# Splitting an attention pair's softmax into three places of the issue order, with two norms applied in other ways

## The reference

```
h  = rms(x) * ln1_g * (1 + sc1) + sh1;   u = h @ w_in
fox: 8 heads of 64:  logit = q.k/8 + cum[t] - cum[s], causal; softmax; @ v      (cum: running sum of log sigmoid)
diff: 4 heads:       (softmax(q1 k1 + alibi) - lam * softmax(q2 k2 + alibi)) @ v, then rms over 128
x  = x + g1 * (concat(fox, diff) @ w_out)
h2 = rms(x) * ln2_g * (1 + sc2) + sh2;   x = x + g2 * ((silu(h2 @ w_gate) * (h2 @ w_up)) @ w_down)
```

## Time and profile before

| | us |
|---|---|
| median of 3 runs | 817.25 |
| the profiled execution, whole | 818.92 |
| its span, first to last instruction | 817.2 |
| PE busy, matmuls | 775.0 (95%) |
| DVE busy | 466.4 (57%) |
| ACT busy | 390.6 (48%) |
| POOL busy | 59.4 (7%) |

### The profile page before, as it was taken

How to read it: one execution, slowest core, us unless ns; L and a number is a source line. 1 busy time by engine, 2 the same in 40 slices (tenths; PEclk the granted TensorE clock), 3 DMA queues, 4 the chain that set the end, 5 groups by cost and what they waited for, 6 DMA issues and landing times.

```text
span 817.2 us, 10224 instructions
## 1 busy us (share of the span) xinstructions
PE 775.0 (95%) x3955; PEld 616.8 (75%) x3955; DVE 466.4 (57%) x607; ACT 390.6 (48%) x544; POOL 59.4 (7%) x70
## 2 busy tenths in 40 slices
PE   3988899988999999999999999999999999999995
PEld 2667675656888889888878887777888888888884
DVE  3466676747565556464595436555565656545364
ACT  3255666644344334353634356665455545335252
POOL 2004030010000000000280000000010000000001
PEclk9999999999999999999999999999999999999998
DMA  9998336895655347656749464333565645564601
GB/s 275 289 361 274 112 105 254 312 397 195 219 194 184 125 155 232 232 180 203 255 162 331 155 205 154 105 104 111 170 194 162 200 156 201 164 201 154 206 26 51
DMA packets 86785, 158.73 MB, mean 194 GB/s; under 512 B 5226, under 2 KB 23875, under 8 KB 84690
## 3 DMA queue, kind: packets, MB, share of 16 engines
q1 hardware_dynamic: 84562, 151.16, 55.7%
q0 software_dynamic: 2128, 6.90, 2.7%
q10 hardware_dynamic: 48, 0.01, 0.0%
HBM read 156.99 MB, written 1.08 MB: 193 GB/s over the span
## 4 chain that ended last, share of the span: by engine, by line
PE 82%; DVE 5%; issue 3%; SPq 3%; ACT 3%; DMA 2%; POOL 1%; DVEq 0%; POOLq 0%; ACTq 0%
PE PS L872 25%; PE PS L874 24%; PE PS L873 24%; PE PS L986 3%; DMA raw<-in_w_ada 2%; PE PS L1066 1%; ACT whi L1165 1%; PE PS L960 1%; DVE wlo L1377 1%; PE PS L1037 1%; SPq L802 1%; PE PS L1092 1%; PE PS L1021 1%; SPq L790 1%; POOL hrs L1780 1%
## 5 line engine op out<-in xcount | busy, mean ns | idle before, releaser
L1377 DVE TENSOR_TENSOR wlo<-raw,whi 128x2048 fp32r<-128x2048 f32 (+1 forms) x126 | 280.2, 2226 | 190.4 <-ACT whi L1165 162.4
L1165 ACT ACTIVATE whi<-raw 128x2048 fp32r<-128x2048 f32 (+1 forms) x126 | 227.1, 1804 | 156.2 <-PE PS L874 156.2
L872 PE MATMUL PS<-whi,hT 128*128 128x512 f32 (+1 forms) x704 | 280.6, 399 | 2.2 <-issue 1.9
L874 PE MATMUL PS<-whi,hT 128*128 128x512 f32 (+1 forms) x704 | 272.8, 388 | 0.0
L873 PE MATMUL PS<-wlo,hT 128*128 128x512 f32 (+1 forms) x704 | 272.7, 387 | 0.0
L872 PEld LDWEIGHTS PS<-whi,hT 128*128 128x128 f32 x704 | 133.5, 190 | 33.1 <-issue 8.4
L874 PEld LDWEIGHTS PS<-whi,hT 128*128 128x128 f32 x704 | 133.3, 189 | 27.5
L873 PEld LDWEIGHTS PS<-wlo,hT 128*128 128x128 f32 x704 | 133.7, 190 | 23.9
L872 PE MATMUL PS<-whi,hidT 128*128 128x512 f32 x216 | 84.5, 391 | 0.0
L874 PE MATMUL PS<-whi,hidT 128*128 128x512 f32 x216 | 84.1, 389 | 0.0
L873 PE MATMUL PS<-wlo,hidT 128*128 128x512 f32 x216 | 84.1, 389 | 0.0
(11 more groups left out here) (227 smaller groups left out, 643.7 us busy)
## 6 DMA issues: line engine op xcount, KB each, us to landing
raw<-in_w_in SPq DMA_DIRECT2D x36, 1024.0 KB, 5.1
raw<-in_w_ff SPq DMA_DIRECT2D x32, 1024.0 KB, 5.2
raw<-in_w_ada SPq DMA_DIRECT2D x16, 1024.0 KB, 6.9
raw<-in_w_gate SPq DMA_DIRECT2D x10, 1024.0 KB, 5.4
raw<-in_w_up SPq DMA_DIRECT2D x10, 1024.0 KB, 5.1
raw<-in_w_down SPq DMA_DIRECT2D x10, 1024.0 KB, 5.2
raw<-in_w_ada SPq DMA_DIRECT2D x16, 512.0 KB, 7.2
raw<-in_w_out SPq DMA_DIRECT2D x8, 1024.0 KB, 5.1
```

Source lines behind the costliest of these rows:

```text
L872: pe.matmul(o, ah, wh, start=(k == 0), stop=False)
L874: return pe.matmul(o, al, wh, start=False, stop=end)
L1165: act.activation(split_view(whi, i), slab_view(raw, slot, i), ACT.Copy).then_inc(hi_made, 1)
L1377: dve.tensor_tensor(split_view(wlo, i), slab_view(raw, slot, i), whole(split_view(whi, i)), ALU.subtract).then_inc(lo_made, 1)
```

## The change

1. A pair's `scores` step is cut in three. The maxima stay in `scores`; the exponentials on ACT become `exp u+1`, which is put behind `probsT u` (in fox behind its first head) and ahead of `heads u+2`; the reciprocals and the scaling on DVE become `probs u`, which is put at the front of pair u, ahead of `scores u+1`. For pair 0, `exp` stands behind `heads 1`.
2. The row constant `cumq` is gone: the `cum` step with its transposes and copy, and L1588 and L1589.
3. `lam` moves from behind `heads 1` to ahead of the forget gate.
4. The diff norm is done for heads 0 and 1 at the end of pair 6, and for heads 2 and 3 at the end of pair 7. The first `turn` stands directly behind pair 7.
5. Norm 1: POOL makes the root per half of the tokens, DVE scales the identity by it (`diag`), and PE multiplies x by `diag`, which transposes and scales in one; `xnb` is no longer made. `mod` is done in two parts, the first inside the output projection.
6. One slab's split is moved from the output projection to behind the last `turn` of norm 1.

The diff at its core (the rest declares and removes names, and counts `norm_rs` one lower):

```diff
@@ -140,17 +140,25 @@
         for u in us:
             moba, c = kind_of(u) == "moba", BETWEEN.get(u, BETWEEN[kind_of(u)])
 
+            out += [("probs", u)]
             if u != us[-1]:
                 out += [("scores", u + 1)]
             if moba and u != us[0]:
                 out += [("back", u - 1)]
-            out += fill(c[0]) + [("probsT", (u, 0))] + ([("probsT", (u, 1))] if moba else []) + fill(c[1])
+            out += fill(c[0]) + [("probsT", (u, 0))] + ([("probsT", (u, 1))] if moba else [])
+            if u != us[-1]:
+                out += [("exp", u + 1)]
+            out += fill(c[1])
             if u + 2 <= us[-1]:
                 out += [("heads", u + 2)]
             out += fill(c[2])
             if kind_of(u) == "fox":
                 out += [("probsT", (u, 1))] + fill(c[3])
             out += [("values", u)] + fill(c[4])
+            if u == FOX_P + 2:
+                out += [("diffnorm", 0)]
+            if u == FOX_P + 3:
+                out += [("diffnorm", 1)] + turns("diff", 0, (0,))
...
-    order += early + [("fgate", 0), ("unit", 0), ("logf", 0), ("unit", 1)]
+    order += early + [("lam", 0), ("fgate", 0), ("unit", 0), ("logf", 0), ("unit", 1)]
     now = whole("fox", 2, "w_in", 2 * W, "h")
-    order += insert(now, (4, early), (5, [("cum", 0)]), (6, [("heads", 0)]))
+    order += insert(now, (4, early), (6, [("heads", 0)]))
...
-    order += [("scores", 0), ("heads", 1), ("lam", 0)] + tail[:3]
+    order += [("scores", 0), ("heads", 1), ("exp", 0)] + tail[:3]
     tail = tail[3:]
     order += attention(list(range(FOX_P + DIFF_P)), tail, ada[18:20])
-    order += [("diffnorm", 0)] + ada[20:21] + turns("diff", 0, (0, 1)) + ada[21:22]
-    order += slab(wo[0], "w_out", 0, 4) + [("evac", wo[0])]
+    order += ada[20:22] + turns("diff", 0, (1,)) + insert(slab(wo[0], "w_out", 0, 4), (2, [("mod", 1)])) + [("evac", wo[0])]
     order += insert(slab(wo[1], "w_out", W, 4), (1, [("sums", (1, 0))])) + [("evac", wo[1]), ("sums", (1, 1))] + ada[22:24]
-    order += [("mod", 2), ("norm", 1)]
-    order += turns("norm", 1, (0, 1)) + parts("norm", 1, (0, 1)) + turns("norm", 1, (2, 3)) + parts("norm", 1, (2, 3))
+    order += [("norm", 1), ("first", 0), ("mod", 2), ("first", 1)]
+    order += turns("norm", 1, (0, 1)) + parts("norm", 1, (0, 1)) + [("first", 2), ("first", 3)]
+    order += turns("norm", 1, (2, 3)) + [("split", None)] + parts("norm", 1, (2, 3))
...
@@ -265,7 +273,8 @@
             split += 1
             continue
         if it[0] == "piece" and it[1]["first"] and it[1]["slab"] >= KC + 2:
-            while split <= min(it[1]["slab"] + min(2, it[1]["slab"] + 1), len(slabs) - 1):
+            held = tiles[it[1]["T"]]["name"] == "w_out" and it[1]["k"] == 4 and tiles[it[1]["T"]]["n"] == 1
+            while split <= min(it[1]["slab"] + (1 if held else 2), len(slabs) - 1):
                 out.append(("split", split))
...
@@ -965,13 +973,22 @@
 
                 elif kind == "mod":
 
-                    for n, pk in enumerate((1, 2)):
-                        pe.wait_ge(mod_in, pk)
-                        take(4 + n)
-                        for c in range(4):
-                            last = pe.transpose(PS[:, 4 + n, c * P:(c + 1) * P], mod[:, pk, c * P:(c + 1) * P], ident)
+                    pe.wait_ge(mod_in, i)
+                    take(3 + i)
+                    for c in range(4):
+                        last = pe.transpose(PS[:, 3 + i, c * P:(c + 1) * P], mod[:, i, c * P:(c + 1) * P], ident)
                     last.then_inc(mod_T, 1)
-                    reader[4] = reader[5] = [(ab_made, 1)]
+                    reader[3 + i] = [((b2_made, ab_made)[i - 1], 1)]
+
+                elif kind == "first":
+
+                    key = ("norm", 1, i)
+                    b = turn_bank(TURNS[key])
+                    take(b)
+                    pe.wait_ge(diag_made, 1)
+                    for c in range(2):
+                        k = 2 * i + c
+                        pe.matmul(PS[:, b, c * S:c * S + P], x[:, 0, k * P:(k + 1) * P], diag[:, 0, :], start=True, stop=True)
 
...
-                    for c in range(2):
-                        for t in range(TB):
-                            o = c * S + t * P
-                            last = pe.transpose(PS[:, b, o:o + P], src[:, t, c * P:(c + 1) * P], ident)
+                    if is_affine(i):
+                        for c in range(2):
+                            last = pe.matmul(PS[:, b, c * S + P:(c + 1) * S], src[:, 1, c * P:(c + 1) * P], diag[:, 1, :],
+                                             start=True, stop=True)
...
+                    dve.wait_ge(norm_rs, 1)
+                    dve.tensor_scalar(xn1[:, 1, :], x[:, 1, :], nrs[:, 0, 1:2], None, ALU.mult).then_inc(xn_dve, 1)
+
+                elif kind == "norm" and i == 1:
+                    for t in range(TB):
+                        dve.wait_ge(rs1_made, t + 1)
+                        dve.tensor_scalar(diag[:, t, :], ident, nrs[:, 1, t:t + 1], None, ALU.mult).then_inc(diag_made, 1)
...
                                 dve.wait_ge(setup_in, 16 * NSETUP)
-                                dve.wait_ge(cumq_in, 1)
-                            if a >= 2:
-                                dve.wait_ge(smax, 2 * (a - 2) + 2)
-                            dve.tensor_scalar(mcum[:, a % 2, 0:P], mask[:, P:2 * P], cumq[:, 0, a:a + 1], None, ALU.add)
-                            dve.tensor_scalar(mcum[:, a % 2, P:3 * P], mask, cumq[:, 1, a:a + 1], None, ALU.add
-                                              ).then_inc(mcum_in, 1)
-                            dve.wait_ge(mcum_in, a + 1)
-                            bias = [mcum[:, a % 2, c0:c1] for c0, c1 in QB]
+                            bias = [mask[:, P:2 * P], mask]
...
                             dve.tensor_tensor_reduce(made, score, bias[t], -1.0, 3e38,
                                                      ALU.add, ALU.min, nmax[:, a, t:t + 1]).then_inc(smax, 1)
+
+                elif kind == "probs":
+                    u, kd, sc = i, kind_of(i), scores_sb(i)
                     for n in range(2):
...
 
                 elif kind == "diffnorm":
-                    dve.wait_ge(drs_made, 1)
-                    dve.wait_ge(od_in, DIFF)
-                    o = od.rearrange("p t (h d) -> p (t h) d", h=DIFF)
-                    dve.tensor_tensor(o, o, spread(drs[:, :], P), ALU.mult).then_inc(od_made, 1)
+                    dve.wait_ge(drs_made, i + 1)
+                    dve.wait_ge(od_in, 2 * i + 2)
+                    o = od[:, :, i * 2 * P:(i + 1) * 2 * P].rearrange("p t (h d) -> p t h d", h=2)
+                    rs = drs[:, 2 * TB * i:2 * TB * (i + 1)].rearrange("p (h t) -> p t h", h=2)
...
@@ -1809,6 +1820,13 @@
 
                 elif kind == "norm":
                     n = i
+                    if n == 1:
+                        for t in range(TB):
+                            pool.wait_ge(sums_made, 3 + t)
+                            then(pool.tensor_tensor(nss[:, 1, t:t + 1, 0], nss[:, 1, t:t + 1, 0], nss[:, 1, t:t + 1, 1], ALU.add))
+                            last = inverse_root(nrs[:, 1, t:t + 1], nss[:, 1, t:t + 1, 0], D)
+                            last.then_inc(rs1_made, 1)
+                        continue
                     if n:
...
@@ -1866,8 +1884,9 @@
                                    ).then_inc((g1_row, g2_row)[i], 16)
 
                 elif kind == "diffnorm":
-                    pool.wait_ge(dsq_in, DIFF)
-                    inverse_root(drs[:, :], dss[:, :], 2 * HD).then_inc(drs_made, 1)
+                    c = slice(2 * TB * i, 2 * TB * (i + 1))
+                    pool.wait_ge(dsq_in, 2 * i + 2)
+                    inverse_root(drs[:, c], dss[:, c], 2 * HD).then_inc(drs_made, 1)
 
```

69 lines of the change are left out of this document (31 added, 38 removed).

## The result

The changed kernel took 828.36 us (826.86 to 828.71, 4 runs) against 817.74 us (817.03 to 818.62, 4 runs): a ratio of 1.0126, 95% interval 1.0108 to 1.0143, or +10.3 us (8.8 to 11.7) on 817.25. The forecast was 829.3 us, in a range of 818.5 to 836; its +12.05 us lies 0.4 us above the upper end of that interval. The profiled executions took 828.39 us (span 826.6) and 818.92 us (span 817.2): +9.4 us of span.

What follows compares the result with a forecast made beforehand. TensorE's waits, some 12 us with the clock's falls, held all the change could win; DVE's and ACT's queues set the loss. Terms summed to +12.0 us on 818.92; less 1.67 for the median, 829.3 us, range 818.5 to 836.

Steps and rivals of the forecast that it cites:

- queue terms: Pairs 2 to 7: delays in ACT's and DVE's queues, +1.3, +3.6, +0.8 and +6.45 us, 12.15 in all.
- POOL chain: Before pair 7's transposes: the diff norm's root waits behind `grow`'s read, then scaling and normalisation; transposes at 172.6 us.
- The exponentials in front of the heads, +12.2 us: Pairs 2 to 7: 1.87 us of exponentials on ACT, now ahead of the heads' copies, delay TensorE; bounds 0 and 15.
- Fox pairs, +0.7: Pairs 1 and 2: normalisation in front of the maxima outweighs the dropped mask sums, +0.4 and +0.35 us.
- -0.3: Pair 0's first transposes: stay about as late, with exponentials behind `heads 1`, row constant gone, normalisation before the maxima; -0.3 us.
- Lam: Forget gate: `lam`'s 0.80 us stands before the scaling that `heads 0` needs; stall 4.0 us instead of 2.6.
- Norm 1: Norm 1: product with `diag` starts earlier, against 1.8 us more work, about half beside DVE; -1.0 us, bounds -2 and +1.
- The clock: Before pair 7's transposes: a new 2.6 us stall may make the clock fall; +0.85 us, half of 1.65.
- rival of the page's rule: Whole kernel: no clock fall anywhere from the new stalls; 827.2 us, chance 0.08.
- the queues have slack: ACT from pair 2's first copy to `scores 7`: exponentials fall into idle time; 816.25 us, or 813.5; chance 0.10.
- half of it: Pairs 3 to 7: chain through POOL not met, slab's split not waiting for ACT, no fall; 823.4 us, chance 0.20.
- more falls: Pairs 2, 4, 5 and 6: three further clock falls show in full after 2 us stalls; 834.2 us, chance 0.12.

Runs made afterwards that it cites:

- e1: The changed kernel with the exponentials back directly behind their maxima, in front of the copy `pt`, in all pairs; 820.78 us, ratio 1.0038.
- e4: The kernel before with only the row constant taken out; 814.18 us, ratio 0.9957.
- e3: The changed kernel with maxima, exponentials and normalisation of a pair together again, all other edits kept; 811.18 us, ratio 0.9913 to the kernel before.
- e5: e3 with `lam` put back behind heads 1; 810.43 us, ratio 0.9898 to the kernel before.
- e7: e3 with norm 1 by scaled copies and 16 transposes again; 812.53 us, ratio 0.9920 to the kernel before.
- e9: The changed kernel with the diff norm of heads 0 and 1 behind pair 7's normalisation; 822.1 us, ratio 1.0061 to the kernel before.
- e11: e3 with the diff norm's first transposes one `ada` group later, and heads 0 and scores 0 behind more pieces; 811.08 us, ratio 0.9906.

## Why the prediction was right, and where its parts were not

By place, predicted against the drift of the trace:

| stretch | predicted | measured |
|---|---|---|
| start, to the forget gate's product | 0 | -0.6 |
| from there to pair 0's transposes | +0.9 | +1.3 |
| fox, to pair 2's second transposes | +0.7 | +0.3 |
| from there to pair 7's values, clock included | +13.0 | +12.2 |
| diff norm, transposes | -2.4 | -2.9 |
| norm 1 | -1.0 | -0.8 |
| feed-forward to the end, moba included | +0.8 | -0.1 |
| sum | +12.0 | +9.4 |

**The queue terms** held nearly stall by stall: values 2 +1.0 (1.3 predicted), pair 3 +3.2 (3.6), scores 7 and pair 6 as said (waits of 1.7 and 1.9 us). The POOL chain is the clearest: from the end of the read's issue to pair 7's transposes the prediction had 4.1 us (168.5 to 172.6); the rows above have 179.33 - 175.26 = 4.07. One sign failed: the wait before pair 7's transposes was to be over 2 us and was 1.04. The clock was low from pair 6's transposes on (0.57 over 172 to 176 us), so TensorE came later to a point that POOL's chain had fixed, and part of that wait was spent in slower products.

**The step that was mislabelled** is "The exponentials in front of the heads, +12.2 us. This is the heart of it". Its working already held the normalisation in front of the maxima (1.95 us at pairs 4 and 6), but its name gave all to the exponentials. By that e1 would have run at 815.5 us; it ran at 820.8. Each move alone costs 9 to 10 us, and undoing one leaves most of the other.

**The small terms hid large ones.** "Fox pairs, +0.7" and "-0.3" for pair 0 netted the row constant's gain against the normalisation's cost. e4 shows the gain alone, 3.5 us. So the order costs 17.4 us and the other edits win 7.1 (the row constant 3.5, the diff norm's halves 1.7, the rest within what the runs separate), where the sum by place made it look like one loss of 12 and a few small items. The order's cost also starts earlier than the prediction's heart of it: by pair 2's first transposes the changed kernel is 5.8 us behind e3 (127.05 against 121.25), most of it a wait of 2.41 us and a fall of the clock at pair 0, where e3 has neither. The total came out because places don't ask which edit they belong to.

**Lam**: +0.8 us before heads 0 was about right (a wait of 4.0 us predicted and 3.97 measured, and 3.23 in e5 without `lam`), but the other end was left out: behind heads 1 `lam` stalled ScalarE in front of `whi` (e5), and its removal from there makes up for it, as far as the times can tell.

**Norm 1**: the extra work of the products was right (16 take 3.8 us in e3's trace against 1.94 for transposes in e7, +1.9, where 1.8 was predicted; rows at the end), though one product and one transpose were each priced too high, at 0.28 and 0.17 us against 0.24 and 0.12. More than the predicted half of it is covered by work beside it: e3's feed-forward starts within 0.2 us of e7's (188.15 and 188.03). By the Trainium skill ("TensorE: Matmul & The Clock Gate", section "Terms") it would have been a factor of four; the traces give two.

**The clock** was sized at +0.85. The changed kernel's profile has two more falls in pairs 4 to 7 than before, and one fewer at norm 1, where it had fallen behind the wait of 2.06 us. From the transposes of pair 0 to the scores of pair 6 the changed kernel's profile lost 2.55 us against e9's with the same waits up to there, 1.6 behind pair 0's and 1.0 behind pair 4's. So falls between two waits were in part covered, as the prediction had it, and its +0.85 came by another stall than the one that it named: pair 7's wait was 1.04 us and no fall followed it. The rival of the page's rule (827.2 us) lies nearer to the measured 827.6 than the forecast does, but its mechanism is refuted: the section "Why this matters for your kernels" of the Trainium skill's page would let it fall only behind the wait of 4.0 us, and it fell behind 2.4, 1.97 and 1.94 us too. Its price was mis-worked as well: the 1.2 us that it takes off are the forget gate's, whose fall stands behind the one wait for which the rule allows it; 829.3 - 0.85 = 828.45 would have been its time. The rivals "the queues have slack", "half of it" and "more falls" gave 816, 823 and 834; the interval (826.1 to 828.9) excludes them; the forecast's own 829.3 is 0.4 us outside it.

## What to carry to other kernels

In a program with in-order engines, price a moved step by what is queued behind it on its own engine, not by the step: 1.9 us of exponentials, moved past one copy, delayed what TensorE and VectorE waited for at pair 0 and from pair 2 to pair 7, and nothing that could be measured in the moba pairs. A sum by place came near the time here; only undoing each edit alone tells which edit earned or lost it, since gains and losses at one place net out. And a wait that seems worth filling (e11, e5) often only guards a chain on another engine; look for the chain's next consumer before moving work into it.
